# The first pair of each feed-forward: from seven products of sums to eight plain products

## What is computed

```python
def swiglu_ffn(h, g, w_in, w_out):
    gate, up = jnp.split(rmsnorm(h, g) @ w_in, 2, axis=-1)
    return (jax.nn.silu(gate) * up) @ w_out
...
    h = h + 0.5 * swiglu_ffn(h, p['ffn1_g'][layer], ...)
    h = h + y                        # the mixer
    h = h + 0.5 * swiglu_ffn(h, p['ffn2_g'][layer], ...)
```

## Time and profile before

| | us |
|---|---|
| median of 3 runs | 2572.82 (2571.29 to 2572.9) |
| the profiled execution | 2572.65 |
| its span, first to last instruction | 2571.0 |
| TensorE busy | 2449.6 (95%) |
| VectorE busy | 1706.7 (66%) |
| ScalarE busy | 1005.8 (39%) |
| GpSimd busy | 215.1 (8%) |

### The profile page before, as it was taken

The page is one execution under the profiler, slowest core; times in us unless marked ns, Lnnn a source line. Parts: engine busy times, 40 slices in busy tenths (PEclk is TensorE's granted clock), DMA queues, the critical chain, the costliest instruction groups (busy, mean ns, idle before and its releaser), DMA issues.

```text
span 2571.0 us, 44255 instructions
## 1 busy us (share of the span) xinstructions
PE 2449.6 (95%) x17740; PEld 2364.3 (92%) x17740; DVE 1706.7 (66%) x2793; ACT 1005.8 (39%) x1856; POOL 215.1 (8%) x178
## 2 busy tenths in 40 slices
PE   5999999999999995999999998999999997999997
PEld 4999999989898985999999998999998787999997
DVE  6858587554646458858587368677676768758574
ACT  4625353121313133525343235344343544526252
POOL 0000003211111102000002210000012011000002
PEclk8999999999999997999999999999999998999998
DMA  3323332322222212323333433233323431333231
GB/s 109 98 82 91 91 87 83 90 66 70 90 68 81 76 56 59 91 83 93 88 89 85 142 86 99 84 90 90 91 79 107 119 86 51 90 91 92 83 88 62
DMA packets 394749, 222.11 MB, mean 86 GB/s; under 512 B 9105, under 2 KB 387057, under 8 KB 394577
## 3 DMA queue, kind: packets, MB, share of 16 engines
q1 hardware_dynamic: 389840, 205.22, 27.7%
q0 software_dynamic: 4544, 14.50, 1.7%
q10 hardware_dynamic: 192, 0.04, 0.0%
HBM read 206.01 MB, written 13.71 MB: 85 GB/s over the span
## 4 chain that ended last, share of the span: by engine, by line
PE 85%; DVE 9%; ACT 3%; issue 2%; DMA 1%; POOL 0%; ACTq 0%; DVEq 0%; SPq 0%; POOLq 0%
PE ps L2009 40%; PE ps L2072 37%; DVE wl L730 2%; DVE wl L749 1%; PE ps L2464 1%; PE ps L2275 1%; PE ps L2261 1%; PE ps L2262 1%; PE ps L2263 1%; DVE ws L766 1%; PE ps L2492 1%; PE ps L2516 1%; DVE h L1331 1%; DVE xl L1217 1%; DVE up L1329 0%
## 5 line engine op out<-in xcount | busy, mean ns | idle before, releaser
L730 DVE TENSOR_TENSOR wl<-raw,wh 128x1024 fp32r<-128x1024 f32 (+2 forms) x208 | 252.7, 1215 | 467.4 <-ACT wh L725 467.3
L2072 PE MATMUL ps<-xh,wl 128*128 128x288 f32 x1408 | 421.5, 299 | 34.0 <-DVE wl L749 23.1
L725 ACT CAST wh<-raw 128x1024 fp32r<-128x1024 f32 (+2 forms) x208 | 197.6, 950 | 588.8 <-PE ps L2009 588.7
L2072 PE MATMUL ps<-xh,wh 128*128 128x288 f32 x1408 | 420.2, 298 | 0.0
L2072 PE MATMUL ps<-xl,wh 128*128 128x288 f32 x1408 | 419.7, 298 | 0.0
L2072 PE MATMUL ps<-xmh,wl 128*128 128x288 f32 x1056 | 317.7, 301 | 34.7 <-DVE up L1367 20.0
L2072 PE MATMUL ps<-xmh,wh 128*128 128x288 f32 x1056 | 316.7, 300 | 0.0
L2072 PE MATMUL ps<-xml,wh 128*128 128x288 f32 x1056 | 316.2, 299 | 0.0
L2009 PE MATMUL ps<-acth,wl 128*128 128x288 f32 x1408 | 304.2, 297 | 0.3
L2072 PEld LDWEIGHTS ps<-xh,wl 128*128 128x128 f32 x1408 | 269.2, 191 | 37.8 <-DVE wl L749 23.9
L2009 PE MATMUL ps<-actl,wh 128*128 128x288 f32 x1408 | 302.7, 296 | 0.0
(11 more groups left out here) (296 smaller groups left out, 4317.5 us busy)
## 6 DMA issues: line engine op xcount, KB each, us to landing
raw<-in_ffn_w_in SPq DMA_DIRECT2D x176, 512.0 KB, 3.8
raw<-in_ffn_w_out SPq DMA_DIRECT2D x64, 512.0 KB, 3.6
raw<-in_ret_w_in SPq DMA_DIRECT2D x48, 512.0 KB, 3.8
raw<-in_ffn_w_out SPq DMA_DIRECT2D x32, 384.0 KB, 3.2
raw<-in_ret_w_out SPq DMA_DIRECT2D x32, 256.0 KB, 2.8
raw<-in_fox_w_kvf SPq DMA_DIRECT2D x16, 512.0 KB, 4.1
raw<-in_fox_w_q SPq DMA_DIRECT2D x8, 512.0 KB, 4.9
bias<-cum_scratch SPq DMA_DIRECT2D x16, 256.0 KB, 3.4
```

The source lines that it names most:

```text
L725: nc.scalar.copy(slot(wh, s, kt), raw[:, s, 0:kt, :]).then_inc(hi_ready, 1)
L730: nc.vector.tensor_tensor(slot(wl, s, kt), raw[:, s, 0:kt, :], slot(wh, s, kt).bitcast(F32), ALU.subtract).then_inc(lo_ready, 1)
L2072: mm = nc.tensor.matmul(out, w, x, start=begins and q == 0 and m == 0, stop=q == QUADS - 1 and m == 2, skip_group_check=not begins)
```

## The change

The first pair of each feed-forward (g = KF * n) is no longer formed of seven products but row by row: `plain_pair` on TensorE runs gate, then up, each as 8 blocks over all 576 columns like an output unit, from two 1024-wide weight splits (`pair_hi`, `pair_lo`). x is split plainly for it (`x_plain`). The sums of x, the weight factors of the second pair, the roots of the norm and the differences x_apart are made in a new step, `enter`, whose instructions stand behind the pair splits. x_apart overwrites the second column half of xh[0..3], so it waits for both rows (pair_done). `add_up` and p1 are gone; the first row is multiplied by rstd out of PSUM at the end of `enter`, the second copied from there by ScalarE. `spread_apart` stands after G11 of the second pair and writes to another bank, the sums of the squares come between the two rows. In ffn1_1 the sums of x are made during the v section as before; in ffn2_1 three of four are made between the outputs. In ffn1_0 the five squares stand together before `enter`. Counters go by `done(g)`, as one pair in 22 has no factors.

```diff
+        def pair_hi(act, n, row):
+            g, units = KF * n, opening[KF * n]
+            if units:
+                act.wait_ge(unit_done, units - 1 + row)
+            act.wait_ge(pair_in[(2 * g + row) % RAW], 16 * (g // 2 + 1))
+            nc.scalar.copy(slot(wh, row, KD), raw[:, (2 * g + row) % RAW, :, :]).then_inc(pair_hi_ready, 1)
+        def pair_lo(dve, n, row):
+            g = KF * n
+            dve.wait_ge(pair_hi_ready, 2 * n + row + 1)
+            nc.vector.tensor_tensor(slot(wl, row, KD), raw[:, (2 * g + row) % RAW, :, :], slot(wh, row, KD).bitcast(F32),
+                                    ALU.subtract).then_inc(pair_lo_ready, 1)
...
@@ ScalarE
+            def x_apart(n, q):
+                act.wait_ge(pair_done, 2 * n + 2)
+                act.wait_ge(mixed, mixed_at(n, "apart", q))
+                nc.scalar.activation(xh[:, q, TA:T], apart_x[:, q % 2, :], ACT.Copy, scale=gain_of(n, q)).then_inc(xfhi_ready, 1)
+            def enter(n, pairs):
+                g = KF * n + 1
+                for q in pairs:
+                    x_sums(n, q)
+                    if q + 2 < QUADS:
+                        x_scaled(n, q + 2)
+                    if q == pairs[min(1, len(pairs) - 1)]:
+                        factor_hi(act, g, G11)
+                if not pairs:
+                    factor_hi(act, g, G11)
+                for i in (DIF, S2, G12, S1):
+                    factor_hi(act, g, i)
+                for q in range(QUADS):
+                    x_apart(n, q)
+                act.wait_ge(pair_done, 2 * n + 2)
+                nc.scalar.copy(up[:, 0, :], pair_psum(2)).then_inc(up_ready, 1)
...
-            squares(0, 2)
-            ffn("ffn1_0", G_MIX, between=lambda: squares(2, TT))
+            squares(0, TT)
+            enter(0, range(QUADS))
+            ffn("ffn1_0", G_MIX)
...
@@ VectorE
+            def enter(n, pairs, roots=None):
+                g = KF * n + 1
+                for q in pairs[:2]:
+                    x_mix(n, q)
+                    x_sums(n, q)
+                weight_sums(dve, g, (S1, DIF, S2))
+                factor_lo(dve, g, G11)
+                for q in pairs[2:]:
+                    x_mix(n, q)
+                    x_sums(n, q)
+                factor_lo(dve, g, DIF)
+                if roots is not None:
+                    roots()
+                factor_lo(dve, g, S2)
+                weight_sums(dve, g, (S4,))
+                factor_lo(dve, g, G12)
+                if roots is not None:
+                    take_rstd_apart()
+                factor_lo(dve, g, S1)
+                x_apart(n, 0)
+                x_apart(n, 1)
+                for q in range(QUADS):
+                    x_apart_lo(n, q)
+                    if q + 2 < QUADS:
+                        x_apart(n, q + 2)
+                dve.wait_ge(pair_done, 2 * n + 1)
+                nc.vector.tensor_tensor(gate[:, 0, :], pair_psum(0), rstd[:, :], ALU.mult).then_inc(gate_ready, 1)
...
@@ VectorE, output of the last head (ffn2_0)
-                if n >= KD - 3:
-                    lead_lo(dve, group0["ffn2_0", 0], n - KD + 3)
                 take_h(u, n, n, 1.0, None, DEEP)
-                x_lo(1, n)
+                if n == KD - 1:
+                    pair_lo(dve, 1, 0)
+                    pair_lo(dve, 1, 1)
+                if n:
+                    x_plain(1, n - 1)
+            x_plain(1, KD - 1)
+            enter(1, range(QUADS), lambda: token_rstd(6))
...
@@ VectorE, fox_out (ffn2_1)
+                if n < APART:
+                    x_plain(3, n)
+                if QUADS <= n < KD - 1:
+                    x_mix(3, n - QUADS)
+                    x_sums(3, n - QUADS)
+                if n == KD - 1:
+                    for j in range(APART, KD):
+                        x_plain(3, j)
+            def first_row(eng, g, which):
+                if which == 2:
+                    pair_lo(eng, 3, 0)
+            section(dve, "fox_out", split_lo, take_fox, lead=first_row)
+            pair_lo(dve, 3, 1)
+            enter(3, (3,), lambda: token_rstd(6))
...
@@ TensorE
+            def plain_pair(n, units, norm, turn, midway):
+                for row in range(2):
+                    if units:
+                        pe.wait_ge(taken, units if n == 2 and row else units - 1)
+                    pe.wait_ge(pair_lo_ready, 2 * n + row + 1)
+                    for k in range(KD):
+                        if row == 0:
+                            if turn is not None:
+                                turn(k)
+                            pe.wait_ge(xfactor_ready, x_at[n, "plain", k])
+                        e = KD * row + k
+                        mm = product(pair_psum(2 * row), ((wl[:, e, :], xh[:, k, :]), (wh[:, e, :], xl[:, k, :]),
+                                                          (wh[:, e, :], xh[:, k, :])), k == 0, k == KD - 1)
+                    mm.then_inc(pair_done, 1)
+                    if row == 0 and midway is not None:
+                        midway()
...
+                    plain_pair(n, units, norm, turn, midway)
+                    for i in (G11, DIF, S2, G12, S1):
+                        block_product(n, g0 + 1, 1, i, True)
+                        if i == G11 and norm:
+                            spread_apart()
```

More of the change, by code:

```diff
@@ L172, in encoder @@
         last = g0 + FF_PARTS[part][1] - 1
-        comes(g0, (G11, DIF, S2, G12, S1) if g0 else (G11, S1, DIF, S2, G12))
-        for g in range(g0, last + 1):
+        a0 = g0 + (part == 0)
+        comes(a0, (G11, DIF, S2, G12, S1))
+        for g in range(a0, last + 1):
             more = (g + 1,) if g < last else ()
-            comes(g, (S1,) if g > g0 else ())
+            comes(g, (S1,) if g > a0 else ())
             for a in more:
@@ L530, in x_factor_at @@
         def x_factor_at(n, i, q):
[L531 to L537, removed]
-        def mixed_at(n, kind, q):
[L541 to L547, removed]
+            return x_at[n, "sums" if i in (DIF, S2, U22) else "apart" if i == S1 else "plain",
+                        q + QUADS if i in (G12, S4) else q]
+        def mixed_at(n, kind, q):
+            return 4 * QUADS * n + (3 * q + 3 if kind == "sums" else 3 * QUADS + q + 1)
         def sums_at(g, i):
-            return 4 * g + SUMS.index(i) + 1
+            return 4 * (done(g) - 1) + SUMS.index(i) + 1
         def v_low(t):
@@ L914, in ffn @@
+                        act.wait_ge(made[G11], done(g))
+                        if g >= 2:
+                            act.wait_ge(gate_ready, g - 1)
+                        nc.scalar.copy(bank(g, S2), bank(g, G11)).then_inc(seeded1, 1)
+                        if more:
+                            factor_hi(act, g + 1, G11)
+                            factor_hi(act, g + 1, DIF)
+                        if g == g0 + 2 and part == 0 and entry is not None:
                             entry()
-                        if i >= 2:
+                        if g >= g0 + 2:
@@ L1760, in _ @@
             gate_rows()
-            section(dve, "v", split_lo, take_kv(first["v"], KD), lead=lead_lo)
-            for q in range(QUADS):
-                x_second(2, q)
+            section(dve, "v", split_lo, take_kv(first["v"], KD))
+            x_plain(2, KD - 1)
+            pair_lo(dve, 2, 1)
+            enter(2, ())
             def kv_out():
@@ L2096, in group @@
                     block_product(n, g - before, 1 - b if before else b, i)
-                    if second is not None and i == DIF:
-                        second()
-            def factors(name, part, norm=False, arrives=None, midway=None):
+            def plain_pair(n, units, norm, turn, midway):
[14 more added lines that the diff above has]
+                        midway()
```

410 lines of the change are left out of this document (157 added, 253 removed).

## The result

| | us |
|---|---|
| kernel before, median | 2572.86 (2571.29 to 2576.73) |
| changed kernel, median | 2545.24 (2542.68 to 2546.65) |
| ratio | 0.9889, 95% interval 0.9872 to 0.9906 |
| profiled execution of the changed kernel | 2544.5, span 2542.8 |

A forecast was written before the change was run, and what follows sets the result against it. VectorE's queue was taken to bound the feed-forward entries. Gains of 0.6, 11.5, 11.9 and 4.0 us sum to 28.0, added products included: 2572.65 - 28.0 = 2544.65, given as 2544.5 us, range 2536 to 2556.

The forecast's parts named there:

- What bounds the kernel: At the feed-forward entries TensorE runs dry waiting for VectorE's queue: VectorE busy 64.18 of 82.40 us up to 1037.30.
- The added products: First pair of each feed-forward takes 96 products instead of 84: 6.4 us over four entries, all on TensorE's path.
- The cover: Sums, factors, roots and x_apart come beside the first pair's rows, whose 96 products give 12.8 us of cover.
- The walks: Step-by-step timing of each entry to the third pair's G11: gains 0.6, 11.5, 11.9 and 4.0 us.
- The squares: GpSimd's squares in ffn2_0 and ffn2_1 slow VectorE instructions with two SBUF operands, by 1.1 us each.
- The 2547.5 beside the sum: Total if each such VectorE instruction waited out a whole 1.5 us square: about 3 us less gain in ffn2_0.
- Dearer handoffs: First rival: some 25 handoffs between engines per entry each cost 0.1 us more, 10 us: 2554.5; chance 0.20.
- Squares that hold nobody up: Second rival: squares don't delay VectorE; 6 us earlier in ffn2_0, 9 in ffn2_1: 2529.5; chance 0.07.
- The clock: Third rival, slower: rows and second pair stay at 1.2 GHz in all four entries, 42 us more: 2586; chance 0.05.
- Waits that only move: Fourth rival: row 0 starts dry in first and third entry, tail longer in all; gain 3 us, 2569.6; chance 0.03.
- The milestone: Start of the third pair's G11, taken as the point from which both kernels have the same work left.

The follow-up runs named there:

- a_products: Changed kernel plus 24 unused products (3.2 us at full clock) on TensorE between the second row and G11 in each of four entries; 2552.79 us.
- b_work: Changed kernel plus five unread subtractions on VectorE ahead of x_apart in each entry (estimate 3.0 us together); 2558.75 us.
- b_order: Changed kernel with, in ffn2_0 alone, the sums of x 0 and 1 made before the two pair splits, not beside the rows; 2544.29 us.
- b_squares: Changed kernel with, in ffn1_0 alone, ScalarE's five squares made between the casts of the sums of x, not ahead of the first; 2539.44 us.
- a_base: The changed kernel run again, unedited, as base for the other runs; median 2544.45 us.
- a_seed: Changed kernel with the copy seeding S2 ahead of the four x_apart in ScalarE's queue, that seeding S1 ahead of the second row's copy; 2542.71 us.
- b_pool: Changed kernel with GpSimd's squares before ffn2_0 and ffn2_1 cut to 64 of 576 columns (first square whole), so another norm there; 2533.40 us.
- c_psum: Changed kernel with, in ffn2_0 alone, ScalarE's four squares added up by TensorE between the two rows, not by GpSimd; 2541.07 us.

## Why the prediction was right, point by point

**What bounds the kernel: right for ffn2_0.** The experiments tell of the changed kernel; of the one before there are only the traces. Three views agree: 3.2 us on TensorE are free in ffn1_0 and ffn2_0 (a_products), 3.0 on VectorE cost 3.5 and 3.0 (b_work), and 13 us of delay of row 0 cost nothing (b_order). In ffn1_1, 3.2 us on TensorE cost 1.9 and 3.0 on VectorE 2.1: each has about 1 us to spare there, so VectorE's queue alone is not the bound of this entry. In ffn2_1 both cost something (2.1 and 1.8, up to 1.8 more by the slow first trace); the order of the code has the chain run through both engines there (rows, spread, rstd, tail).

**The added products: the term was wrong.** 6.4 us were put "all on TensorE's path". a_products shows that products stand on the path in two entries of four. The sum did not suffer, since it was made by walking each entry and not by adding this term; but the term gives a false picture of where the price is paid.

**The cover: wrong as a reason in ffn2_0.** The 12.8 us of rows were named as what hides sums and factors. By b_order two of the four sums can stand ahead of the rows as well. In this entry VectorE has less to do for a first pair (two pair splits, in place of seven low factors, four weight sums and what add_up took): it is busy for 8.0 us less in the stretch and idle for 3.0 less, 11.0 together. In the other entries its saving and the gain lie far apart. In ffn1_0 4.9 us less work won nothing: VectorE then waited 5.0 us for ScalarE, whose five squares stood ahead of its cast, and b_squares got 3.7 of it back. In ffn1_1 5.4 us less went with 12.0 won, where TensorE's short waits disappeared; here the new order may well count, but no run tests it. In ffn2_1 9.7 us less work won 4.1, as VectorE stood idle for 5.6 more. Nor does any run keep the seven products and change their place alone, so how the gain divides between the plain form and the new order is not shown.

**The walks: right to 1 us at nearly every step.**

| step | predicted | measured |
|---|---|---|
| ffn1_0: G11, spread (roots done), S2 | 42.6, 53.6, 62.2 | 42.83, 53.74, 62.34 |
| ffn1_0: third G11 | 68.5 | 69.34 |
| ffn2_0: idle before row 0, spread, S2 | 4.4, 9.4, 3.5 | 3.2, 8.9, 3.2 |
| ffn2_0: third G11 | 1025.8 | 1025.34 |
| ffn1_1: idle before S2 | 0.8 | 0.66 |
| ffn2_1: idle before row 0, before S2 | 7.5, 5.2 | 6.9, 4.5 |
| gains | 0.6, 11.5, 11.9, 4.0 | -0.2, 11.0, 12.0, 4.1 |

In ffn1_0 the 0.8 us are the clock: the 36 products from S2 to the third G11 take 7.0 us at a granted clock of 0.66, S2 alone 3.0 of them. In ffn2_0 the walk began at 954.92, and the changed kernel was there 0.9 us sooner.

**The squares: the size right, the reading wrong.** 1.1 us on each slowed instruction was close: the two splits cost 1.1 each on top. But the prediction took its rows to speak against whole squares being waited out, which is a misreading. In the earlier trace rows too the ends alternate: 981.29 (VectorE), 982.54 (GpSimd), 983.09 (VectorE). GpSimd's 1.79 us hold its own wait; a square alone takes 1.15 (at 979.21 above). So the whole instruction is waited out, and it costs about the 1.1 that the sum used. The 2547.5 beside the sum came from 1.5 us for each.

**The rivals.** Dearer handoffs: the walks leave no room for 0.1 us more on each. Squares that hold nobody up: their premise is false, but their size was nearly right: without most of the squares' work the kernel is 11 us faster, against the 15 that this rival named. The clock: 0.81, 0.86, 1.00 and 0.88 in the four stretches, so what was feared did not happen; ffn1_1 never left the upper level. Waits that only move: four of them did (row 0, spread, S2, G11), but none was dearer than counted.

**Luck in the total.** That the profiled execution took 2544.5 us to the tenth is chance. The entries won 26.8 us, the span 28.2. The steps outside them (-0.3, 1.5, -3.0, 1.5 and 1.7 in order) belong to code that the change leaves alone; they might as well have summed to -3. The same kernel's profiled execution in a_base took 2539.84.

**The milestone was too early.** Third G11 is no point from which nothing more is lost: in a_seed it came 5.1 us sooner and the stretch behind it gave 4 us back. VectorE's addition of up in the second pair would have been the better one.

## What to carry to other kernels

Where a stretch is bound by one engine's queue, work taken from that queue is the first estimate of the gain, but for that stretch alone, and only if the other engines' waits are walked through too. Here 5 to 10 us less of VectorE's work in an entry went with anything from nothing to 12 us won, and that the totals agree (28.0 and 28.2) is a sum of misses that cancel. To find the bound, put the same 3 us on either engine and see which costs. A long wait of the busiest engine says who is late, not that moving the waiting work will help: moving the spread, the seeds and row 0 all left the end nearly where it was. And every relief has a point from which another engine takes over: in ffn2_0 it came at 4.7 of 8.8 us, and was seen as a wait in the opposite direction.

## What the runs showed of the hardware

**The same idle times, another clock.** At about 1410 us both kernels run the same code with the same VectorE times. Granted clock (third number from the end) of the 8 us ahead of a wait and of the 37 products behind it, first before, then the changed kernel:

```profile
1411.00:1419.00 8.00, 7.35 (x42) 7.15 (x42) 6.27 (x6) 2.49 (x3) 4.58 (x4) 0.79 0.49 129
...
1421.60:1426.46 4.86, 4.86 (x37) 4.86 (x37) 3.80 (x18) 0.00 (x0) 0.18 (x1) 1.00 0.50 123
```

```profile
1399.05:1407.05 8.00, 5.81 (x42) 5.61 (x42) 6.28 (x6) 2.49 (x3) 4.59 (x4) 1.00 0.50 130
...
1410.50:1417.54 7.04, 7.04 (x37) 7.04 (x37) 3.00 (x18) 0.00 (x0) 0.00 (x0) 0.65 0.29 76
```

Before, the lower level falls ahead of the wait, where VectorE is late anyway and slow products cost nothing: TensorE's busy time grows into its idle time. Changed, it falls behind the wait and costs 2.2 us there and 0.8 in the 17 products in between. The two traces of the changed kernel differ at this place by 3 us in the same way. So a place like this gives or takes 1.5 to 3 us by chance, and one profile against another can't tell an edit's 2 us outside the stretch that it touches. Such places lie at about 950, 1410 and 1955 us in this kernel; inside ffn2_1, row 0 took 9.1 us in one trace and 7.9 in the other.

**Column sums are dear.** A column sum with one column of output shows as two matmuls in the trace and takes 0.22 to 0.24 us at full clock (five between 2114.18 and 2115.27 us in b_pool, five between 990.51 and 991.70 in the changed kernel), nearly what two of the 288-wide products take. 20 more of them, meant as a small price, are 4.6 us by this (an estimate), and were 6.5 in c_psum.
